# Root mean square norms applied after the products instead of before them, in a two-block model on one core

## The reference, cut to what matters

```
def rms_norm_2(x, g):
    y = x * rsqrt(mean(x * x, axis=-1) + EPS)
    return y * g
...
    x = x + gt2 * conv_ffn(h, ...)                  # first block
    h = rms_norm(x, norm_f_w)                       # enters the second block
    xn = rms_norm_2(h, norm_mix[0]); proj = xn @ w_in_even
    y_a = a_b * causal_dwconv3(a_c * a_v, conv_a)
    y_b = pooled(z_b) @ w_pool * pool_scale         # moving means of 2, 4, 8, 16 tokens, minus z_b
    h = h + concat(y_a, y_b) @ w_out_even
    h = h + gated_conv_ffn(rms_norm_2(h, norm_ffn[0]), ...)
    proj = gelu(rms_norm_2(h, norm_mix[1]) @ w_in_odd); u, v = halves(proj)
    h = h + (u * spatial_gate(rms_norm_2(v, sgu_norm))) @ w_out_odd
    h = h + gated_conv_ffn(rms_norm_2(h, norm_ffn[1]), ...)
    return rms_norm_2(h, final_norm)
# gated_conv_ffn(x): (silu(causal_dwconv3(x @ w_gate) + conv_b) * (x @ w_up)) @ w_down
```

## Time and profile before

| | us |
|---|---|
| median of three runs | 2682.74 |
| profiled execution | 2683.41 |
| its span, first to last instruction | 2682.1 |
| TensorE matmul busy | 2471.5 (92%) |
| VectorE busy | 1129.0 (42%) |
| ScalarE busy | 694.7 (26%) |
| GpSimd busy | 931.1 (35%) |

### The profile page before, as it was taken

How to read it: one execution, slowest core, us unless ns; L and a number is a source line. 1 busy time by engine, 2 the same in 40 slices (tenths; PEclk the granted TensorE clock), 3 DMA queues, 4 the chain that set the end, 5 groups by cost and what they waited for, 6 DMA issues and landing times.

```text
span 2682.1 us, 29295 instructions
## 1 busy us (share of the span) xinstructions
PE 2471.5 (92%) x12190; PEld 1930.5 (72%) x12190; DVE 1129.0 (42%) x1676; ACT 694.7 (26%) x863; POOL 931.1 (35%) x430
## 2 busy tenths in 40 slices
PE   5999998999998899799999787899999978899997
PEld 3777775777777687588888465688887656688886
DVE  3121234677775313666642355433311127333311
ACT  3122113333332321222221311322211331322212
POOL 4322221111110443344444242445444422444442
PEclk7999998999998899899999898899999898899998
DMA  5433332211111333233332122233331412233331
GB/s 200 128 101 107 114 95 61 46 41 43 33 38 42 95 94 84 65 99 94 97 110 84 43 63 80 65 101 95 104 104 45 117 55 63 65 101 94 112 98 42
DMA packets 412021, 222.28 MB, mean 83 GB/s; under 512 B 33823, under 2 KB 409458, under 8 KB 410610
## 3 DMA queue, kind: packets, MB, share of 16 engines
q1 hardware_dynamic: 387394, 208.28, 26.8%
q10 hardware_dynamic: 24496, 12.13, 1.7%
HBM read 214.61 MB, written 5.77 MB: 82 GB/s over the span
## 4 chain that ended last, share of the span: by engine, by line
PE 60%; DVE 4%; ACT 1%; POOL 1%; issue 0%; DVEq 0%; POOLq 0%
PE bank L311 59%; POOL h_low L520 1%; DVE sq L509 1%; PE bank L314 1%; ACT L481 0%; ACT h_high L530 0%; DVE ev_s L2148 0%; DVE ev_s L2150 0%; DVE od_vn L2296 0%; DVE sq L513 0%; DVE x_res L497 0%; DVE rinv L473 0%; DVE od_low L2300 0%; DVE od_vn L2292 0%; ACT rinv L481 0%
## 5 line engine op out<-in xcount | busy, mean ns | idle before, releaser
L307 POOL TENSOR_TENSOR w_low<-w_raw,w_high 128x1024 fp32r<-128x1024 f32 (+1 forms) x331 | 864.0, 2612 | 1534.3 <-ACT w_high L300 1534.3
L311 PE MATMUL bank<-h_high,w_high 128*128 128x512 f32 x2008 | 823.5, 410 | 70.6 <-DVE h_low L520 45.8
L311 PE MATMUL bank<-h_low,w_high 128*128 128x512 f32 x2008 | 799.3, 398 | 0.0
L300 ACT CAST w_high<-w_raw 128x1024 fp32r<-128x1024 f32 (+1 forms) x331 | 359.5, 1087 | 1107.6 <-PE bank L311 1090.2
L311 PEld LDWEIGHTS bank<-h_high,w_high 128*128 128x128 f32 x2008 | 385.8, 192 | 204.9 <-issue 66.8
L311 PE MATMUL bank<-h_high,w_low 128*128 128x512 f32 x2008 | 516.1, 397 | 0.0
L311 PEld LDWEIGHTS bank<-h_low,w_high 128*128 128x128 f32 x2008 | 388.2, 193 | 77.1 <-issue 3.0
L311 PEld LDWEIGHTS bank<-h_high,w_low 128*128 128x128 f32 x2008 | 382.2, 191 | 84.2 <-issue 3.4
L311 PE MATMUL bank<-g_high,w_high 128*128 128x512 f32 x352 | 139.1, 395 | 0.0
L311 PE MATMUL bank<-g_low,w_high 128*128 128x512 f32 x352 | 139.0, 395 | 0.0
L1951 DVE TENSOR_TENSOR x_res<-bank,x_res 128x512 f32<-128x512 f32 x32 | 22.1, 692 | 237.8 <-PE bank L311 237.8
(11 more groups left out here) (322 smaller groups left out, 2799.3 us busy)
## 6 DMA issues: line engine op xcount, KB each, us to landing
w_raw<-in_w_in SPq DMA_DIRECT2D x58, 512.0 KB, 4.9
w_raw<-in_w_up SPq DMA_DIRECT2D x44, 512.0 KB, 3.8
w_raw<-in_w_ffn_gate SPq DMA_DIRECT2D x44, 512.0 KB, 3.8
w_raw<-in_w_ffn_up SPq DMA_DIRECT2D x44, 512.0 KB, 3.8
w_raw<-in_w_ffn_down SPq DMA_DIRECT2D x32, 704.0 KB, 4.5
w_raw<-in_w_ada SPq DMA_DIRECT2D x32, 512.0 KB, 3.8
w_raw<-in_w_down SPq DMA_DIRECT2D x16, 704.0 KB, 4.5
w_raw<-in_w_in ACTq DMA_DIRECT2D x21, 512.0 KB, 4.1
```

The source lines that it names most:

```text
L300: self.A.copy(self.w_high[:, u % SPLIT_SLOTS, 0:k * P], self.raw_of(key)[:, 0:k * P]).then_inc(*self.S.rounded(*key))
L307: self.G.tensor_tensor(self.w_low[:, slot, 0:k * P], self.raw_of(key)[:, 0:k * P], self.w_high[:, slot, 0:k * P].bitcast(F32), ALU.subtrac ...
L311: return self.T.matmul(out, lhsT, rhs, start=start, stop=stop, skip_group_check=True)
```

## The change

Between a projection and the next stage no norm stands any more, for the norms named `even`, `gated0`, `odd`, `gated1` and the final one. (`ffn`, which has a shift, keeps the old form.) After each output tile of the projection is added to `x`, VectorE multiplies it by the gain alone (into `sq[:, 1]`), ScalarE rounds that to `h_high`, and VectorE subtracts to get `h_low`; GpSimd has no share in it. So the next stage's products work on `x` times gain, and the sum over the partitions comes after that stage's first product, with the root behind it. The banks are no longer cleared of their old users at the start of a stage.

What takes the results scales them by the root. In the gated feed-forward (`ffn_ahead_dve`) VectorE makes a scaled copy of the gate product and the scaled last tap from PSUM, then adds the other taps from the scaled copy in SBUF; the bias goes into Silu; the up product is scaled into SBUF before it is multiplied. In the odd layer VectorE scales each product into `uv`, and Gelu works on `uv` in place. In the even layer the four pool products come first; the roots of both norms are taken after the first of them (`rinv_first` for the first, then the second, whose sum of squares is multiplied twice by `rinv_first`); `e_root` is their product, `e_square` its square. VectorE scales the pool products, prepares the counts, scales the eight tiles of `x` by `rinv_first`, and then for each of the four groups does the pool chain (`pool_dve`), the gated convolution with its root and square, and the mixed pool result. TensorE does the product with `w_pool` after each group of three products, and waits there for the pool chain. The ring follows that order, with `w_pool` after each three. In `f_down` VectorE also squares for the first norm and multiplies `x` by `norm_f_w` (`first`).

At the end the final gain is multiplied into `x` in the last projection, the root is taken with tokens on the partitions (four small products, 128x4 values), `x` is transposed while it is taken, and ScalarE and VectorE each scale half of every block of rows.

```diff
+        for g in range(4):
+            unit(("pool", g), even, 12 * P + g * P)
         for n in range(4):
             for j in (1, 2, 0):
                 unit(("even", n, j), even, n * P + j * 4 * P)
-        for g in range(4):
-            unit(("pool", g), even, 12 * P + g * P)
-            if g == 3:
-                unit(("even_out", 0, 0), split("w_out_even_2"), 0)
-            ring.append((("w_pool", g), [(0, 0, None, io["w_pool_2"][0, g])], None))
-        for n in range(1, DT):
+            ring.append((("w_pool", n), [(0, 0, None, io["w_pool_2"][0, n])], None))
+        for n in range(DT):
...
+    def project_act(self, name, outputs, following, to):
+        rounds = [(name, n, k0) for n, k0, _ in outputs[1:]] + ([following] if following else [])
+        self.round_unit(rounds[0])
+        for m, (n, k0, _) in enumerate(outputs):
+            if m + 1 < len(rounds):
+                self.round_unit(rounds[m + 1])
+            if to and (m + 1 == len(outputs) or outputs[m + 1][0] != n):
+                self.A.wait_ge(*self.S.dve_norm.at(to, "gained", n))
+                self.A.copy(self.h_high[:, n, :], self.sq[:, 1, :]).then_inc(*self.S.act_norm(to, "high", n))
...
+        if first:
+            V.memset(self.rinv_first[:], 0.0).then_inc(*S_.dve_norm())
...
+            if to:
+                V.tensor_scalar(gained, x, gain(n), None, ALU.mult).then_inc(*S_.dve_norm(to, "gained", n))
+            if first:
+                self.add_square(self.rinv_first, x)
+                V.tensor_scalar(x, x, first(n), None, ALU.mult).then_inc(*S_.dve_norm())
+                V.wait_ge(*self.own("dve"))
+            self.add_square(self.rinv, x, name, "squares", n)
+            if gain and not to:
+                V.tensor_scalar(x, x, gain(n), None, ALU.mult).then_inc(*S_.residual("gained", n))
+            if to:
+                V.wait_ge(*S_.act_norm.at(to, "high", n))
+                V.tensor_tensor(self.h_low[:, n, :], gained, self.h_high[:, n, :].bitcast(F32),
+                                ALU.subtract).then_inc(*S_.h_low_even(to, n))
+    def add_square(self, total, x, *key):
+        V, square = self.V, self.sq[:, 0, :]
+        V.tensor_tensor(square, x, x, ALU.mult).then_inc(*self.S.dve_norm())
+        V.wait_ge(*self.own("dve"))
+        V.tensor_tensor(total[:], total[:], square, ALU.add).then_inc(*self.S.dve_norm(*key))
+    def ahead(self, name):
+        return lambda k: [self.S.h_low_even.at(name, k)]
+    def root_ahead_pe(self, name, before, first=False):
+        T, S_ = self.T, self.S
+        T.wait_ge(*S_.dve_norm.at(before, "squares", DT - 1))
+        for b, total, key in ((6, self.rinv_first if first else None, "first"), (7, self.rinv, "sum")):
+            if total is not None:
+                self.empty(b)
+                self.mm(self.bank[b][:], self.ones[:], total[:], True, True).then_inc(*S_.norm_sum(name, key))
+                self.emptied[b] = (S_.dve_norm, (name, "mean" if key == "sum" else "mean first"))
+    def root_ahead_dve(self, name):
+        V, S_ = self.V, self.S
+        V.wait_ge(*S_.norm_sum.at(name, "sum"))
+        V.tensor_scalar(self.rinv[:], self.bank[7][:], 1.0 / D, RMS_EPS, ALU.mult, ALU.add).then_inc(*S_.dve_norm(name, "mean"))
...
+                    if before and n == 0:
+                        self.root_act(norm)
+                        A.activation(self.spare[:], self.ones[:, 0:1], ACT.Silu).then_inc(*S_.silu())
...
+    def ffn_ahead_dve(self, name, norm, taps):
+        V, S_ = self.V, self.S
+        self.root_ahead_dve(norm)
+        V.wait_ge(*S_.act_norm.at(norm, "root"))
+        for n in range(FT):
+            gate, scaled = self.f_c[:, n % 2, 0, :], self.f_c[:, n % 2, 1, :]
+            bank = self.bank[2 * (n % 2)]
+            tap = [taps(0, a)[:, n:n + 1] for a in range(3)]
+            V.wait_ge(*S_.product.at(name, n, 0))
+            V.wait_ge(*self.own("dve"))
+            V.tensor_tensor(scaled, bank[:], self.rinv[:], ALU.mult).then_inc(*S_.parts())
+            V.scalar_tensor_tensor(gate, bank[:], tap[2], self.rinv[:], ALU.mult, ALU.mult).then_inc(*S_.parts("taken", name, n, 0))
+            V.wait_ge(*self.own("dve"))
+            V.scalar_tensor_tensor(gate[:, 1:S], scaled[:, 0:S - 1], tap[1], gate[:, 1:S], ALU.mult, ALU.add).then_inc(*S_.parts())
+            V.wait_ge(*self.own("dve"))
+            V.scalar_tensor_tensor(gate[:, 2:S], scaled[:, 0:S - 2], tap[0], gate[:, 2:S], ALU.mult,
+                                   ALU.add).then_inc(*S_.conv(name, n, 0))
+            V.wait_ge(*S_.product.at(name, n, 1))
+            V.wait_ge(*self.own("dve"))
+            V.tensor_tensor(scaled, self.bank[2 * (n % 2) + 1][:], self.rinv[:], ALU.mult).then_inc(*S_.parts("taken", name, n, 1))
+            V.wait_ge(*S_.silu.at(name, n))
+            V.wait_ge(*self.own("dve"))
+            V.tensor_tensor(gate, gate, scaled, ALU.mult).then_inc(*S_.parts())
+            V.wait_ge(*self.own("dve"))
+            V.tensor_copy(self.f_high[:, n, :], gate).then_inc(*S_.parts())
+            V.wait_ge(*self.own("dve"))
+            V.tensor_tensor(self.f_low[:, n, :], gate, self.f_high[:, n, :].bitcast(F32), ALU.subtract).then_inc(*S_.parts(name, n))
...
+    def even_pe(self, norm, before):
         T, S_ = self.T, self.S
-        ready = self.h_ready(norm)
-        self.emptied = [None] * 8
+        for g in range(4):
+            self.empty(g)
+            self.product(("pool", g), self.bank[g][:], *self.h_parts(), ready=None if g else self.ahead(norm))
+            self.emptied[g] = (S_.dve_even, ("zp", g))
+            if g == 0:
+                self.root_ahead_pe(norm, before, True)
         for n in range(4):
             for m, j in enumerate(self.EVEN_PARTS):
-                b = 3 * (n % 2) + m
+                b = 4 + m if n % 2 else m
                 self.empty(b)
-                self.product(("even", n, j), self.bank[b][:], *self.h_parts(), ready=ready)
-                ready = None
+                self.product(("even", n, j), self.bank[b][:], *self.h_parts())
...
+            T.wait_ge(*S_.dve_even.at("pooled", n))
+            T.wait_ge(*self.loaded(("w_pool", n)))
+            self.empty(7)
...
+            self.round_unit(after[g + 1])
+            if g == 1:
+                self.roots_act_twice(norm)
...
+        V.wait_ge(*S_.norm_sum.at(norm, "first"))
+        V.tensor_scalar(self.rinv_first[:], self.bank[6][:], 1.0 / D, RMS_EPS, ALU.mult, ALU.add).then_inc(*S_.dve_norm(norm, "mean first"))
+        V.wait_ge(*S_.act_norm.at(norm, "first"))
+        V.wait_ge(*S_.norm_sum.at(norm, "sum"))
+        V.tensor_tensor(self.rinv[:], self.bank[7][:], self.rinv_first[:], ALU.mult).then_inc(*S_.dve_norm(norm, "sum taken"))
+        V.wait_ge(*self.own("dve"))
+        V.tensor_tensor(self.rinv[:], self.rinv[:], self.rinv_first[:], ALU.mult).then_inc(*S_.dve_norm())
+        V.wait_ge(*self.own("dve"))
+        V.tensor_scalar(self.rinv[:], self.rinv[:], 1.0 / D, RMS_EPS, ALU.mult, ALU.add).then_inc(*S_.dve_norm(norm, "mean"))
+        V.wait_ge(*S_.act_norm.at(norm, "root"))
+        V.tensor_tensor(self.e_root[:], self.rinv[:], self.rinv_first[:], ALU.mult).then_inc(*S_.dve_even())
+        V.wait_ge(*self.own("dve"))
+        for g in range(4):
+            V.wait_ge(*S_.product.at("pool", g))
+            V.tensor_tensor(self.e_zp[:, g, :], self.bank[g][:], self.e_root[:], ALU.mult).then_inc(*S_.dve_even("zp", g))
+        V.tensor_tensor(self.e_square[:], self.e_root[:], self.e_root[:], ALU.mult).then_inc(*S_.dve_even())
+        V.wait_ge(*S_.pool_setup.at("positions"))
+        for g, window in enumerate(POOL_WINDOWS):
+            cnt = self.e_cnt[:, g, :]
+            V.tensor_scalar(cnt, self.e_posf[:], float(window), None, ALU.min).then_inc(*S_.dve_even())
+            V.wait_ge(*self.own("dve"))
+            V.reciprocal(cnt[:, 0:window], cnt[:, 0:window]).then_inc(*S_.dve_even())
+            V.memset(cnt[:, window:S], 1.0 / window).then_inc(*S_.dve_even())
+        for k in range(DT):
+            V.tensor_tensor(self.x[:, k, :], self.x[:, k, :], self.rinv_first[:], ALU.mult).then_inc(*S_.dve_even("residual", k))
         for n in range(4):
+            self.pool_dve(n)
             z, c = self.e_z[:, n % 2, :], self.e_c[:, n % 2, :]
-            value, gate = (self.bank[3 * (n % 2) + m] for m in (1, 2))
+            value, gate = (self.even_bank(n, m) for m in (1, 2))
...
+            V.tensor_tensor(z, z, self.e_square[:], ALU.mult).then_inc(*S_.dve_even())
+            V.wait_ge(*self.own("dve"))
+            V.scalar_tensor_tensor(c, z, tap[2], self.e_root[:], ALU.mult, ALU.mult).then_inc(*S_.dve_even())
+            V.wait_ge(*self.own("dve"))
+            V.scalar_tensor_tensor(self.e_s1[:, 1:S], z[:, 0:S - 1], tap[1], self.e_root[:, 1:S], ALU.mult,
+                                   ALU.mult).then_inc(*S_.dve_even())
```

(39 more changed lines are left out.)

260 lines of the change are left out of this document (119 added, 141 removed).

## The result

The changed kernel takes 2579.45 us, the median of 4 runs (2577.73 to 2580.65); the kernel before took 2682.68 in the same comparison (4 runs, 2681.44 to 2683.5). The ratio is 0.9609 [0.9598, 0.9621], that is 103 us less. The forecast was 2590 with a range of 2572 to 2609.

A forecast was written before the change was run, and what follows sets the result against it. TensorE was taken as the bound; -35.6 (gated norms) - 44.0 (even layer) - 5.9 + 0.7 (odd layer) - 8.6 (end) = -93.4 us from 2683.41 gave 2590, with an 8-in-10 range of 2572 to 2609.

The forecast's parts named there:

- Norms `gated0` and `gated1`: Norms before the gated stages: second product starts 7.1 us after the projection's end instead of 24.9, -35.6 us for both.
- Work inside the gated stages: Gated stages: VectorE needs 9.7 to 10.3 us per tile of 10.88, extra pass at the end covered; taken as 0.
- The even layer: From the end of `f_down` through the even layer: 161.4 us instead of 205.4, with 17.8 us of TensorE idle; -44.0.
- even-layer rivals: Even layer does not wait: -58, 2576 us, chance 0.15; or waits at every group: -31, 2603 us, chance 0.16.
- Into the odd layer: Start of odd layer: TensorE idles 9.7 us for late weight loads, second product ends at 24.4 instead of 30.3; -5.9.
- The end: After `g1_down`: root at 6.0 us, then the stores set the pace; 13.6 us instead of 22.2, -8.6.
- VectorE as the bound: Rival in the gated stages: a tile takes 11.6 us, 44 tiles cost 32 us, total 2622; chance 0.10.
- The reversal: Rival in the gated stages: four stalls of 2.1 us per tile lose the whole gain, total 2723; chance 0.04.
- the sum: Whole kernel: all terms of the forecast added, -93.4 us, giving 2590.
- inner range: Whole kernel: the forecast case's own range, 2581 to 2599 us, with chance 0.53.

The follow-up runs named there:

- a_odd_early: The changed kernel with the loads of odd units 1 to 4 issued ahead of the two spatial loads on SyncE's queue: 2573.84 us, ratio 0.9589.
- a_extra3: The changed kernel with three more VectorE passes on two SBUF tiles in each of the 44 gated tiles: 2640.37 us, ratio 0.9835.

## Why the prediction came out right

*Norms `gated0` and `gated1`.* The step held within half a microsecond: 24.9 us became 6.6 (forecast 7.1), a gain of 18.3 each. Columns of VectorE's and TensorE's rows as in the earlier trace rows; the last residual, the low part behind it, the sum of squares as TensorE begins it, and VectorE's first step on it:

```profile
1640.04 0.69 DVE L1959 TENSOR_TENSOR x_res<-bank,x_res 128x512 f32<-128x512 f32 x1 [0.26 <-PE bank L309]
1642.49 0.68 DVE L1975 TENSOR_TENSOR h_low<-sq,h_high 128x512 fp32r<-128x512 f32 x1
1646.71 0.69 DVE L2002 TENSOR_SCALAR rinv<-bank 128x512 f32<-128x512 f32 x1 [3.54 <-PE bank L309]
```

```profile
1645.65 1.02 PE L309 MATMUL bank<-rinv,ones 128*128 128x512 f32 x2
```

The low part of tile 7 ends 3.1 us after the residual began, TensorE is not idle for more than 0.2 us where 0.3 to 0.9 were forecast, and the root is made beside the products.

*Work inside the gated stages.* 43 products in 234.1 us are 5.44 each with no wait, and VectorE's run for a tile takes 9.66 us of 10.88 (the rest is its waits for TensorE, 0.69 and 0.53; forecast 9.7 to 10.3, two meetings). Missed: the end of the stage. I wrote that the extra pass is covered there, and priced no meeting in it. The last tap is held up by GpSimd's low part of the first down unit, which is longer than the others (3.71 us in place of 2.4 to 2.5):

```profile
1877.41 3.59 DVE L2083 SCALAR_TENSOR_TENSOR g_c<-g_c,vec 128x510 f32<-128x510 f32 x1
```

```profile
1876.74 3.71 POOL L305 TENSOR_TENSOR w_low<-w_raw,w_high 128x1408 fp32r<-128x1408 f32 x1 [3.20 <-ACT w_high L298]
```

The same tap takes 0.75 us elsewhere. It ends at 1881.00, Silu takes 0.72 behind it, and TensorE, which waits for ScalarE before the down unit, is idle 1.17 us, twice. So this step failed, for 2.3 us. That the tap without the meeting would have been in time (1878.2, and Silu by 1878.9, when TensorE still had work) is read from the rows and was not run.

*The even layer.* The waits forecast were 4.4, 6.2, 2.5 and 4.7, 17.8 in all; measured 4.0, 5.7, 1.8 and 5.9, 17.4 in all. The double matmul after the wait of 5.66 us takes 2.08 us, as it did before after 6.35:

```profile
1487.12 0.79 PE L309 MATMUL bank<-h_high,w_high 128*128 128x512 f32 x1 [4.04 <-DVE h_low L1975]
1531.22 2.08 PE L309 MATMUL bank<-ev_zp,w_raw 128*128 128x512 f32 x2 [5.66 <-DVE ev_zp L2278]
```

Both even-layer rivals are out: it does wait, but not at every group.

*Into the odd layer.* The wait was forecast as 9.7 and measured as 9.7, and the second product ends at 23.7 in place of 24.4. The row and what ScalarE had waited for:

```profile
2019.33 0.76 PE L309 MATMUL bank<-h_high,w_high 128*128 128x512 f32 x1 [9.72 <-ACT w_high L298]
```

```profile
2018.14 1.04 ACT L298 CAST w_high<-w_raw 128x1024 fp32r<-128x1024 f32 x1 [13.28 <-DMA w_raw<-in_w_in_odd]
```

The wait vanishes with the order of the queue in `a_odd_early`.

*The end.* 12.6 us against 13.6. ScalarE's logarithm, table load, exponential and first scaling:

```profile
2567.34 0.20 ACT L2474 ACTIVATE out_root<-out_root 128x4 f32<-128x4 f32 x1 [15.86 <-DVE out_root L2464]
2567.57 1.28 ACT L2476 ACT_TABLE_LOAD   x1
2568.86 0.20 ACT L2476 ACTIVATE out_root<-out_root 128x4 f32<-128x4 f32 x1
2569.10 1.27 ACT L2480 ACTIVATE out_rows<-bank,out_root 128x512 f32<-128x512 f32 x2
```

The root is ready at 5.2 after the end of `g1_down` (forecast 6.0), the first store is issued at 6.1, and from there to the end are 6.6 us (forecast 6.7, stores only). So what was gained on the forecast is gained before the stores. The load between the two functions is there, so keeping it was right: the rule in the Trainium skill, "ScalarE: Activation LUTs", "Table sets: the hidden batching unit", that one set holds both does not describe this trace.

*The rivals.* VectorE as the bound was not reached, 9.66 us a tile; `a_extra3` shows that the mechanism exists and at 12.15 us costs 61 us of the 103. The reversal needed four stalls in a tile, and no kernel showed more than two.

*What the sum left out.* It had no term for placement. At equal placement the edit gives -91.4 us where I forecast -93.4, so the sum is right also without the placement; the other -10.7 come from where two new tiles push the others. That these stayed inside the range was luck, since no term or bound of the forecast stood for them; the total did fall 1.5 us outside the inner range of 2581 to 2599. The rest of the 105.6 between the two spans, 3.5 us, lies before the merge, in the part that varies by more than that between kernels of the same code and placement.

## What to carry to other kernels

A normalisation without a shift can be applied behind the product; what it is worth is the idle time and the slow clock of TensorE before the first products, and each stage must be walked for what is late next (here a DMA queue, a pool chain and a Silu). When a change adds or removes an SBUF tile, look at pieces of matmuls that it does not touch: if they change pace, its time is partly that of the placement, and an unused tile that restores the old starts separates the two. A wait that a trace shows at one place is cheap to remove by order alone: in their own stages the three gave about 3, 9.4 and 5.9 us here. Before a smaller total is put down to a gain that was given back elsewhere, look at whether the later stage also differs between kernels that have no gain ahead of it.
